# Router logits from plain residual rows: the norm, scale and shift are folded into the weights and the result

## The reference

```
x   = x + gt1 * (o @ w_out)                       # 1024 tokens x 1024
r   = rsqrt(mean(x*x) + eps)                      # one number a token
h2  = x * r * norm2_g * (1 + sc2) + sh2           # gs2 = norm2_g * (1 + sc2)
g   = softmax(h2 @ w_rg + b_rg)                   # 4 groups, top 1
e   = softmax of the group's 8 of (h2 @ w_re + b_re)   # 32 experts, top 2
ffn = sum over the token's two experts of w_down(silu(h2 @ w_gate) * (h2 @ w_up))
x   = x + gt2 * ffn ; then a last modulated norm
```

## Time and profile before

| | |
|---|---|
| median of 3 runs | 1117.65 us (1117.15 to 1123.17) |
| profiled execution | 1114.7 us, its span 1112.9 us |
| TensorE busy, mean granted clock | 1009.9 us (91%), 0.956 of full speed |
| VectorE, ScalarE, GpSimd busy | 727.4, 411.0, 193.1 us |
| share of the chain that ended last | PE 67%, DVE 17%, DMA 6% |

### The profile page before, as it was taken

One profiled execution on the slowest core, in us unless ns is written; L12 is line 12 of the kernel. 1 busy time (PEld: TensorE's weight loads), 2 busy tenths in 40 slices (PEclk: granted clock), 3 DMA queues, 4 the chain that ended last, 5 costly groups with the idle time before them and its releaser, 6 DMA issues.

```text
span 1112.9 us, 17713 instructions
## 1 busy us (share of the span) xinstructions
PE 1009.9 (91%) x6898; PEld 882.4 (79%) x6898; DVE 727.4 (65%) x1456; ACT 411.0 (37%) x700; POOL 193.1 (17%) x290
## 2 busy tenths in 40 slices
PE   3898998999989999999899970499999999999997
PEld 3568788988978989889788870499999999999843
DVE  7768579737965969677756657265565655556427
ACT  4554432654454555446623131022122222222322
POOL 0200101000100010000100032333444434341100
PEclk9799999999999999999999985599999999999998
DMA  9733523221521151201921059379989899898074
GB/s 364 209 115 98 174 68 123 78 67 39 152 77 58 58 190 58 96 1 45 363 73 77 39 182 366 59 296 332 358 322 358 333 339 349 322 359 307 28 289 180
DMA packets 85147, 205.80 MB, mean 185 GB/s; under 512 B 17270, under 2 KB 46022, under 8 KB 76892
## 3 DMA queue, kind: packets, MB, share of 16 engines
q1 hardware_dynamic: 63184, 156.27, 38.6%
q0 software_dynamic: 15280, 42.67, 11.5%
q10 hardware_dynamic: 6620, 6.00, 1.6%
HBM read 188.58 MB, written 24.71 MB: 192 GB/s over the span
## 4 chain that ended last, share of the span: by engine, by line
PE 67%; DVE 17%; DMA 6%; issue 5%; ACT 4%; POOL 1%; SPq 0%; ACTq 0%; POOLq 0%; DVEq 0%
PE PS L2047 21%; PE PS L1801 10%; PE PS L1803 10%; PE PS L1802 10%; DVE AT L1329 3%; PE PS L1866 3%; DVE ACC L1154 3%; PE PS L2039 3%; PE PS L2120 2%; DMA AR<-in_w_ada 2%; DMA WF<-in_w_in 2%; DVE WL L1220 1%; PE PS L2017 1%; PE PS L1773 1%; PE PS L1913 1%
## 5 line engine op out<-in xcount | busy, mean ns | idle before, releaser
L2047 PE MATMUL PS<-XGT,WGU 128*128 128x96 f32 x2048 | 236.4, 277 | 0.0
L2047 PEld LDWEIGHTS PS<-XGT,WGU 128*128 128x128 f32 x2048 | 234.8, 194 | 0.1
L1801 PE MATMUL PS<-WH,HT 128*128 128x256 f32 x512 | 147.8, 289 | 5.1 <-ACT GVB L893 3.2
L1802 PE MATMUL PS<-WL,HT 128*128 128x256 f32 x512 | 145.7, 285 | 0.0
L1803 PE MATMUL PS<-WH,HL 128*128 128x256 f32 x512 | 145.6, 284 | 0.0
L1329 DVE COPY_PREDICATED AT<-MASK,PS 128x64 f32<-128x64 uint8 x320 | 72.9, 228 | 66.4 <-PE PS L1877 47.6
L1801 PEld LDWEIGHTS PS<-WH,HT 128*128 128x128 f32 x512 | 99.1, 194 | 8.0 <-issue 8.0
L1802 PEld LDWEIGHTS PS<-WL,HT 128*128 128x128 f32 x512 | 99.2, 194 | 0.0
L1803 PEld LDWEIGHTS PS<-WH,HL 128*128 128x128 f32 x512 | 99.0, 193 | 0.0
L1096 ACT ACTIVATE SIL<-PS 128x192 f32<-128x192 f32 x32 | 10.6, 331 | 227.6 <-PE PS L2047 227.6
L1801 PE MATMUL PS<-HT,WH 128*128 128x512 f32 x192 | 79.1, 412 | 3.9 <-DVE HL L1235 2.9
(11 more groups left out here) (315 smaller groups left out, 2087.7 us busy)
## 6 DMA issues: line engine op xcount, KB each, us to landing
WGU<-in_w_exp_gate SPq DMA_DIRECT2D x32, 1024.0 KB
WGU<-in_w_exp_up SPq DMA_DIRECT2D x32, 1024.0 KB
WDN<-in_w_exp_down SPq DMA_DIRECT2D x32, 1024.0 KB, 5.0
AR<-in_w_ada POOLq DMA_DIRECT2D x32, 512.0 KB, 4.1
WF<-in_w_in SPq DMA_DIRECT2D x28, 512.0 KB, 5.4
AST<-in_w_ada SPq DMA_DIRECT2D x16, 512.0 KB, 8.9
AR<-in_w_ada_final POOLq DMA_DIRECT2D x16, 512.0 KB, 4.4
YG<-expert_rows SPq DMA_DIRECT2D x8, 1024.0 KB, 12.3
```

What stands on the lines that cost most here:

```text
L1801: MM(ps, wh, xh, start=first, stop=False)
L1802: MM(ps, wh, xl, start=False, stop=False)
L2047: last = MM(GU[par][:, col:col + C], WGU[slot][:, m, k, j * P:(j + 1) * P], XGT[:, par, k, :], start=(k == 0), stop=(k == KD - 1))
```

## The change

(x * r * gs2 + sh2) @ W + b is rewritten as r * (x @ (gs2 * W)) + (sh2 @ W + b):

- TensorE transposes X1 itself ("x1T"), and waits for `x1_ready` where it waited for `xn_ready`. The copy out of PSUM (`x1_evac`) is a plain copy, one instruction a half.
- One new job ("rb", 0), eight matmuls with SH2 as a broadcast left side, makes sh2 @ W in all partitions. `router_rows` on VectorE adds it to BR and multiplies WRT by GS2, once.
- `logits_evac` becomes one scalar_tensor_tensor with RR[t] and BR, and waits for `r2`.
- ScalarE still makes XN for the store, and no longer waits for the transposes; both `route_exps` come after the last XN, instead of the first between XN(6) and the square of tile 7.
- `out_order` and VectorE's hand-written order are laid out anew.

```diff
-    out_order = [("wo", 3, 0), ("wo", 3, 1), ("h2T", 0), ("wo", 4, 0), ("lg", 0), ("h2T", 1), ...
+    out_order = [("rb", 0), ("wo", 3, 0), ("x1T", 0), ("wo", 3, 1), ("lg", 0), ("x1T", 1), ...
...
                 if t >= 2:
                     act.wait_ge(xn_st[t % 2], 16 * (t // 2))
-                    act.wait_ge(pj_ready, number[("h2T", t - 2, 1)] + 1)
                 A(XN[:, t % 2, :], X1[:, t, :], ACT.Copy, scale=RR[:, t:t + 1]).then_inc(xn_ready, 1)
-                if t == NT - 2:
-                    route_exps(0)
...
-            route_exps(1)
+            for g in range(2):
+                route_exps(g)
...
-                    V.tensor_tensor(dst, PJ[n % 2].rearrange("p (k n) -> p k n", k=4),
-                                    GS2[:, ks].rearrange("p (k a) -> p k a", a=1).to_broadcast([P, 4, P]),
-                                    ALU.mult).then_inc(pj_free[n % 2], 1)
+                    V.tensor_copy(X1T[:, t % 2, 4 * half:4 * half + 4, :],
+                                  PJ[n % 2].rearrange("p (k n) -> p k n", k=4)).then_inc(pj_free[n % 2], 1)
                     v_.wait_ge(pj_free[n % 2], n // 2 + 1)
-                    V.tensor_tensor(dst, dst, SH2[:, ks].rearrange("p (k a) -> p k a", a=1).to_broadcast([P, 4, P]),
-                                    ALU.add).then_inc(h2_ready, 1)
...
-                V.tensor_tensor(LG[:, t, :], PJ[n % 2][:, 0:W], BR[:], ALU.add).then_inc(pj_free[n % 2], 1)
+                v_.wait_ge(r2, t + 1)
+                V.scalar_tensor_tensor(out=LG[:, t, :], in0=PJ[n % 2][:, 0:W], scalar=RR[:, t:t + 1], in1=BR[:],
+                                       op0=ALU.mult, op1=ALU.add).then_inc(pj_free[n % 2], 1)
                 v_.wait_ge(pj_free[n % 2], n // 2 + 1)
+
+            def router_rows():
+                n = number[("rb", 0)]
+                v_.wait_ge(pj_ready, n + 1)
+                V.tensor_tensor(BR[:], BR[:], PJ[n % 2][:, 0:W], ALU.add).then_inc(pj_free[n % 2], 1)
+                v_.wait_ge(pj_free[n % 2], n // 2 + 1)
+                link(V.tensor_tensor(WRT[:], WRT[:], GS2[:].rearrange("p (k a) -> p k a", a=1).to_broadcast([P, KD, W]),
+                                     ALU.mult))
...
             inverse_root(2)
+            router_rows()
...
+                elif kind == "rb":
+                    pe.wait_ge(wrt_in, 32)
+                    ps = begin(("rb", 0))
+                    for k in range(KD):
+                        last = MM(ps[:, 0:W], SH2[:, k:k + 1].to_broadcast([P, P]), WRT[:, k, :], start=(k == 0), stop=(k == KD - 1))
+                    last.then_inc(pj_ready, 1)
```

More of the change, by code:

```diff
@@ L176, in layer_kernel @@
     for kind, *i in out_order:
-        jobs += [] if kind == "wo" else [(kind, *i, 0), (kind, *i, 1)] if kind == "h2T" else [(kind, *i)]
+        jobs += [] if kind == "wo" else [(kind, *i, 0), (kind, *i, 1)] if kind == "x1T" else [(kind, *i)]
     number = {j: n for n, j in enumerate(jobs)}
@@ L231, in layer_kernel @@
         XN = at("XN", 172, [P, 2, D])
-        H2T = at("H2T", 120, [P, 2, KD, P])
+        X1T = at("X1T", 120, [P, 2, KD, P])
         SQS = at("SQS", 180, [P, D])
@@ L1456, in residual, with x1_evac @@
                     i.then_inc(x1_ready, 1)
-            def h2_evac(t):
+            def x1_evac(t):
                 if t >= 2:
@@ L1573, in _ @@
             inverse_root(2)
-            for half in range(2):
-                residual(3, half)
-            h2_evac(0)
+            router_rows()
+            residual(3, 0)
+            x1_evac(0)
+            residual(3, 1)
+            logits_evac(0)
+            x1_evac(1)
             inverse_root(3)
             residual(4, 0)
-            logits_evac(0)
-            h2_evac(1)
+            logits_evac(1)
+            x1_evac(2)
             residual(4, 1)
-            logits_evac(1)
-            h2_evac(2)
+            logits_evac(2)
+            x1_evac(3)
             inverse_root(4)
             residual(5, 0)
-            logits_evac(2)
-            h2_evac(3)
-            residual(5, 1)
-            inverse_root(5)
             logits_evac(3)
             choose(0)
+            residual(5, 1)
+            x1_evac(4)
+            inverse_root(5)
             residual(6, 0)
-            h2_evac(4)
-            residual(6, 1)
-            inverse_root(6)
+            logits_evac(4)
             ranks(0)
             slots(0)
+            residual(6, 1)
+            x1_evac(5)
+            inverse_root(6)
             residual(7, 0)
-            logits_evac(4)
-            h2_evac(5)
+            logits_evac(5)
+            x1_evac(6)
             residual(7, 1)
-            logits_evac(5)
+            logits_evac(6)
+            x1_evac(7)
             inverse_root(7)
-            h2_evac(6)
-            h2_evac(7)
-            logits_evac(6)
             logits_evac(7)
@@ L1993, in _, with transpose_x1 @@
                     head_transposes(UNITS - 1)
-            def transpose_xn(t):
-                pe.wait_ge(xn_ready, t + 1)
+            def transpose_x1(t):
+                pe.wait_ge(x1_ready, t + 1)
                 for half in range(2):
-                    ps = begin(("h2T", t, half))
+                    ps = begin(("x1T", t, half))
                     for k in range(4):
-                        last = TR(ps[:, k * P:(k + 1) * P], XN[:, t % 2, 4 * half + k::KD], IDENT[:])
+                        last = TR(ps[:, k * P:(k + 1) * P], X1[:, t, 4 * half + k::KD], IDENT[:])
                     last.then_inc(pj_ready, 1)
@@ L2009, in _ @@
                     last.then_inc(wo_ready, 1)
-                elif kind == "h2T":
-                    transpose_xn(i)
+                elif kind == "rb":
[4 more added lines that the diff above has]
+                    last.then_inc(pj_ready, 1)
+                elif kind == "x1T":
+                    transpose_x1(i)
                 elif kind == "lg":
-                    pe.wait_ge(h2_ready, 2 * i + 2)
-                    pe.wait_ge(wrt_in, 32)
+                    for half in range(2):
+                        evacuated(("x1T", i, half))
                     ps = begin(("lg", i))
                     for k in range(KD):
-                        last = MM(ps[:, 0:W], H2T[:, i % 2, k, :], WRT[:, k, :], start=(k == 0), stop=(k == KD - 1))
+                        last = MM(ps[:, 0:W], X1T[:, i % 2, k, :], WRT[:, k, :], start=(k == 0), stop=(k == KD - 1))
                     last.then_inc(pj_ready, 1)
```

13 lines of the change are left out of this document (5 added, 8 removed).

## The result

The changed kernel takes 1123.72 us (median of 20 runs, 1120.29 to 1127.26), the kernel before, run beside it, 1118.45 us (20 runs). The ratio is 1.0046, 95% interval 1.0033 to 1.0059: about 5.1 us slower, inside the 0.5% that was called no change. The profiled span is 1119.5 us against 1112.9, mean granted clock 0.958 against 0.956.

What follows compares the result with a forecast made beforehand. The table's landing (IDX) was the bound, reached by a routing branch (last logits, scatters) and a weights branch. Terms 2.9 + 3.7 + 1.0 delay weights 7.6 us, less 2.8 spare: +4.8 on 1117.65 gives 1122.5 us, range 1114 to 1126.

Steps and rivals of the forecast that it cites:

- Part 5: Expert weights are issued 7.6 us later; the table's read (IDX) waits behind them in SyncE's queue, landing 4.8 us later.
- Part 2: TensorE waits 3.7 us inside x1T(0), near 590 us, until VectorE's router_rows frees the bank that rb wrote.
- Part 4: Tail from the last output-projection matmul to the last logits shrinks from 16.3 to 5.9 us, 10.4 us shorter.
- E: End of the last output-projection matmul, 653.36 us in the kernel before; forecast to come 7.6 us later, at 661.0.
- Part 6: Moving the exponentials to the end of ScalarE's part changes nothing.
- Part 1: New TensorE work ahead of E (rb, logits 5, transposes 6), with a 1.43 us gap gone: together +2.9 us.
- Part 3: TensorE's granted clock falls after the new wait in x1T(0); bounds 0 and 1.7 us, taken as 1.0.
- the spare: Kernel before: how long the weights clear the queue before IDX needs it; 2.8 us, or 4.8 without the last engine.
- C: Rival, 12 in 100: no new wait at x1T(0), weights 2.9 us later; 1117.8 us, no change.
- B: Rival, 13 in 100: weights don't hold IDX, the routing branch alone decides, -2.8 to -3.8 us; 1114.4 us.
- A: Rival, 7 in 100: x1T(0) doesn't wait, table read past the weights, routing 7.5 us earlier; 1110 us.
- D: Rival, 18 in 100: the last scatter lands only when the weights' burst ends, costing the full 7.6 us; 1125.3 us.

## Why the prediction was near, and where it was not

**What held.** *Part 5* is the cause, and shown: the table's landing hangs on the weights' issue and not on the routing branch (44.1 to 45.2 us after it, with IDX issued anywhere from 34.5 to 37.0 us after it), and with 3 MB fewer ahead the read is back at 4.5 us. *Part 2*: 3.48 us were measured for 3.7, with the releaser that was named, and taking its cause away gave the time back. *Part 4*: E + 6.1 for the scaling's start and E + 6.35 for its end, for 5.9; the copies take 0.69 us each, as taken. It had the last logits at full clock since no gap over 1.2 us was left; in two of the other profiles the clock fell around that gap of 1.18 us all the same, and the scaling starts at E + 6.9 and E + 7.7. *Part 6*: nothing, shown with the order put back.

**Part 1, mis-sized.** From the first matmul of the output projection to E it is 106.54 us before and 110.01 with router_rows early, where TensorE's rows show no wait: +3.5 for +2.9. The 0.6 us are in small things. Pass (3, 1) takes 5.56 us as before, but the logits behind it start 0.3 us after its end (595.29), when VectorE's copies of x1T(0) are done at 595.19; and each transpose job of X1 takes 0.98 us where those of XN took 0.93.

**Part 3, a term that is not a constant.** I took 1.0 us between bounds of 0 and 1.7. It is 0 in two executions, 1.6 in two and some 2.4 in one. The 1.0 is near their mean; no execution showed it.

**A wait that I had not seen.** In the profiled execution VectorE starts the scaling of the logits of tile 5 2.30 us after residual(6, 1), though its inputs are there, and TensorE waits 1.85 us for the bank (the view names "remote" as VectorE's releaser here, and TensorE's transposes in the two others). Without it the idle time at this place is 0.29 us. It stands in three of the nine profiles of kernels with the new order (the changed kernel, and two with two experts put off), and not in the others; in one profile of the old order the same tile's logits, there behind residual(7, 1), start after 1.26 us instead of 0.29, where the long tail covers it. The trace names no cause, and I did not find one. What it costs: rb to E is 81.43 us in the changed kernel, 79.38 in a kernel with the same first wait and the same fall of the clock; 2.05 us. Part 1 had no wait ahead of E. The sign "no TensorE wait over 1.5 us between" was about the tail, and held: 1.18 us.

**The routing branch's gain, and the sum.** Where neither the fall nor this wait came, the last scaling stands 119.5 us after the first matmul of the output projection (the kernel with the exponentials first), where it was 122.7 before: the 2.8 us forecast are 3.2. In the profiled execution they are gone (123.1), for there E came 10.5 us later by this count and not 7.6: 3.5 of part 1, 3.3 of the first wait, 1.6 of the clock and 2.05 of the second wait. So the weights were issued at 663.43 and not at 660 to 661. Either way they don't count, as part 5 said: the table waits. They are why IDX was issued at 698.83 and not at 694.6, together with the scatter, which I had left at 6.14 us and which took 7.70. The sum of +4.8 us met +5.1 by the medians. The profile has +6.9, and of those 2.05 are the wait above; the rest is 4.9. That the medians met so closely is in part luck. With each chance term at its mean over the profiles I estimate E at 3.5 + 3.3 + 1.1 + 0.7 = 8.6 us later, a microsecond more than forecast, and the spare below is larger than the 2.8 that were taken, by 0.3 to 1.4 us; the two errors cancel.

Two figures of the prediction are slips. Its upper bound of +6.5 us doesn't follow from its own terms: 2.9 + 3.7 + 1.7 less 2.8 is +5.5, so the likeliest case ends at 1123.2 us and not at 1124.2, and stays under the 5.6 us beyond which it put 15 of its 50 chances. And the profiled execution took 1114.7 us, not 1113.8; no sum rests on it.

**The spare.** Part 5 left open whether the last engine or the others count, 2.8 or 4.8 us of spare. In the kernel before IDX lands 48.3 us after the weights' issue, in the kernels in which the weights decide 44.1 to 45.2. The difference, 3.1 to 4.2 us, is the spare, and lies between the two.

**The mechanism in part 5 was too narrow.** I had IDX waiting for its turn in SyncE's queue. On ScalarE's queue it landed 44.1 us after the weights' issue all the same. So the cause is the bytes that are already with the DMA engines, and not, or not mainly, the place in one queue. What the order of the queues could not have told is shown by putting the bytes off: 4.9 us back. Why the read's packets on q10 don't run for more than three microseconds beside q1's, when larger ones of the same queue did, stays open.

**The rivals.** *C* (no new wait) is refuted by the profile; a kernel made to fulfil its condition gave 0.9989, no change, as C's price had it (1117.8 against 1117.65). *B* is refuted as a forecast by IDX's 9.82 us. *A* needs both the wait and the weights away: only the kernel with two experts put off and router_rows early shows it, 8.4 us under the kernel before by the medians, of which the deferral alone gives 4.6, so that the change's own part is about 4 us where A had 7.5; the profile of that kernel has the second wait and a fall of the clock behind it, the others with router_rows early have neither. *D* was half right. The scatters do land late because of the weights (7.70 us; 2.15 with no weights in flight), and did so before the change. But the last one landed at 697.52, 6.5 us before the weights had drained, not with them; so it is not held until the burst's end, and the full 7.6 us did not come. The Trainium skill (DMA: Bandwidth & Descriptors, Queues, rings and completion order) says that the semaphore's write lands after every earlier write of its DMA engine, across queues; the rows bear out a delay of 4 to 5.5 us under load and no more, so "earlier" does not take in the weights that were queued then.

## What to carry to other kernels

When a shorter chain feeds a small transfer, look at what is in flight at the time at which that transfer will now be issued. Here 10 us were taken out of the tail behind the last pass, but the burst of weights is issued at the last pass too, so the last scatter and the table's read came 10 us deeper into the burst, and most of the gain went there; the rest of the loss was work and waits put ahead of that pass. What frees the bytes is to put off those that nobody needs yet, behind the last small transfer and not between two of them; another queue gave little or nothing of it. And a job that borrows one of two rotating banks must be emptied by an instruction that stands early on its engine: moving one call by one line was worth 6.4 us by the ratios.

## What the runs showed of the hardware

- The indirect scatter of token numbers lands 2.15 us after its issue with the DMA engines free and 6.1 to 7.7 us under the 1 MB loads or just at their end; the table's read of 5,100 small packets in 4.5 us, or 7.6 to 9.9; the indirect gather in 3.9 to 4.3 us, or 7.4 to 8.2.
- A store of 512 KB on the other queue, issued into the same burst, lands in 8.5 us (9.6 in the kernel before), and the three row transfers behind it took 36% of the engines; the read with the small packets, on that same queue, does not start for more than 3 us.
- Around the same wait of 3.48 us, with the same instructions about it, the granted clock fell to 0.50 in three executions and stayed at 1.00 in two. And it fell at much shorter waits: in one profile of the old order (one expert put off) behind 1.42 us, to 0.50 from 650 to 653, in one of the new order (two put off) behind 1.83 us, and with the wait filled around 1.18 us. My rule of the nearest row, no fall after 3.21 us and a fall after 3.95, was no rule.
